# Weight units of the hybrid decoder step split, signalled and released in two parts

## What is computed

```python
def layer(x, ...):
    h = rmsnorm(x, norm_mix)
    q, k, v, g_ret, x_lru, y_lru, g_a, g_b = jnp.split(h @ w_in, IN_SPLITS, axis=-1)
    o, S_new = retention(rope(q), rope(k) * RET_DK ** -0.5, v, S_ret)      # 4 heads, chunked
    ret_branch = (silu(g_ret) * groupnorm(o) * gn_gain) @ w_ret_out
    hl, h_last = rg_lru(causal_conv(x_lru, ...), ...)                      # a scan over time
    lru_branch = (gelu(y_lru) * hl) @ w_lru_out
    x = x + (sigmoid(g_a + b0) * ret_branch + sigmoid(g_b + b1) * lru_branch) @ w_o
    gu = rmsnorm(x, norm_ffn) @ w_gate_up
    return x + (silu(gu[..., :D_FF]) * gu[..., D_FF:]) @ w_down, ...
```

## Time and profile before

| | |
|---|---|
| median of 3 runs | 2520.05 us |
| the profiled execution's own time | 2516.28 us |
| its span in the profile | 2514.3 us |
| TensorE busy with matmuls | 2447.3 us, 97% |
| weight loads on TensorE | 2367.1 us, 94% |
| POOL busy | 1519.6 us, 60% |
| VectorE (DVE) busy | 1213.4 us, 48% |
| ScalarE (ACT) busy | 647.4 us, 26% |
| granted TensorE clock, mean | 0.996 of full speed |

### The profile page before, as it was taken

The page is one execution under the profiler, slowest core; times in us unless marked ns, Lnnn a source line. Parts: engine busy times, 40 slices in busy tenths (PEclk is TensorE's granted clock), DMA queues, the critical chain, the costliest instruction groups (busy, mean ns, idle before and its releaser), DMA issues.

```text
span 2514.3 us, 51834 instructions
## 1 busy us (share of the span) xinstructions
PE 2447.3 (97%) x19636; PEld 2367.1 (94%) x19636; DVE 1213.4 (48%) x1587; ACT 647.4 (26%) x981; POOL 1519.6 (60%) x1265
## 2 busy tenths in 40 slices
PE   7999999999999999999999999999999999999997
PEld 7899989999999999999998989999999999999997
DVE  6745454668644632022347363636786446221223
ACT  2404040446721211011114040413566112100111
POOL 5364536467776666666654545455777666666664
PEclk9999999999999999999999999999999999999998
DMA  5546363522233322332346363635322323223222
GB/s 197 200 147 226 132 237 113 201 86 84 84 97 96 93 92 81 95 92 84 92 159 234 115 240 112 245 126 191 91 77 90 99 92 93 88 84 97 92 83 86
DMA packets 121742, 315.62 MB, mean 126 GB/s; under 512 B 12192, under 2 KB 12960, under 8 KB 121568
## 3 DMA queue, kind: packets, MB, share of 16 engines
q1 hardware_dynamic: 60480, 199.78, 25.4%
q10 hardware_dynamic: 61088, 113.34, 12.8%
HBM read 272.69 MB, written 40.38 MB: 125 GB/s over the span
## 4 chain that ended last, share of the span: by engine, by line
PE 76%; DVE 7%; issue 4%; ACT 3%; DVEq 3%; DMA 3%; ACTq 2%; POOL 1%; POOLq 1%
PE proj L360 46%; PE aux L360 25%; DMA scratch<-in_sret 2%; DVE scratch L1078 2%; PE aux L560 1%; PE aux L534 1%; DVE scratch L988 1%; PE aux L609 1%; POOL w_low L347 1%; POOLq L345 1%; DVE scratch L1136 1%; DMA scratch<-v_rows 1%; ACTq L1338 1%; DVEq L1081 1%; DVEq L996 0%
## 5 line engine op out<-in xcount | busy, mean ns | idle before, releaser
L347 POOL TENSOR_TENSOR w_low<-w_raw,w_high 128x512 fp32r<-128x512 f32 (+2 forms) x840 | 1094.5, 1323 | 62.8 <-issue 1.3
L344 POOL TENSOR_SCALAR w_high<-w_raw 128x1024 fp32r<-128x1024 f32 (+3 forms) x420 | 424.8, 1011 | 907.9 <-PE proj L360 683.0
L360 PE MATMUL proj<-x_high,w_high 128*128 128x260 f32 x2752 | 561.4, 285 | 33.5 <-DVE x_low L751 13.8
L360 PE MATMUL proj<-x_high,w_low 128*128 128x260 f32 x2752 | 555.6, 283 | 0.0
L360 PE MATMUL proj<-x_low,w_high 128*128 128x260 f32 x2752 | 554.8, 283 | 0.0
L360 PEld LDWEIGHTS proj<-x_high,w_high 128*128 128x128 f32 x2752 | 425.5, 189 | 46.0 <-DVE x_low L751 14.2
L360 PEld LDWEIGHTS proj<-x_high,w_low 128*128 128x128 f32 x2752 | 425.4, 189 | 0.0
L360 PEld LDWEIGHTS proj<-x_low,w_high 128*128 128x128 f32 x2752 | 425.1, 189 | 0.0
L360 PE MATMUL proj<-split_scratch,w_high 128*128 128x260 f32 x2544 | 412.3, 284 | 4.4 <-POOL w_low L347 3.3
L360 PEld LDWEIGHTS proj<-split_scratch,w_high 128*128 128x128 f32 x2544 | 348.1, 188 | 13.0 <-issue 5.0
L360 PE MATMUL aux<-x_high,w_high 128*128 128x260 f32 x1344 | 272.0, 283 | 2.6 <-DVE residual L1215 1.4
(11 more groups left out here) (184 smaller groups left out, 2326.3 us busy)
## 6 DMA issues: line engine op xcount, KB each, us to landing
w_raw<-in_wstream SPq DMA_DIRECT2D x252, 512.0 KB, 3.6
scratch<-in_sret ACTq DMA_DIRECT2D x96, 512.0 KB, 6.9
out_ret_s<-scratch ACTq DMA_DIRECT2D x64, 512.0 KB, 3.7
w_raw<-in_wstream SPq DMA_DIRECT2D x72, 448.0 KB, 3.3
w_raw<-in_wstream SPq DMA_DIRECT2D x48, 384.0 KB, 3.0
scratch<-v_rows ACTq DMA_DIRECT2D x64, 256.0 KB, 4.8
w_raw<-in_wstream SPq DMA_DIRECT2D x48, 320.0 KB, 2.8
out_ret_p<-scratch ACTq DMA_DIRECT2D x8, 512.0 KB, 3.4
```

What stands on the lines that cost most here:

```text
L344: pool.tensor_scalar(WH[:, j, w], WR[:, j, w], 1.0, 0.0, ALU.mult, ALU.add)
L347: m = pool.tensor_tensor(WL[:, j, part], WR[:, j, part], WH[:, j, part].bitcast(F32), ALU.subtract)
L360: m = pe.matmul(out, wt[:, w, blk * P:(blk + 1) * P], x[xi], start=first and n == 0, stop=last and n == 2)
```

## The change

Each unit is cut after its first four blocks (`CUT`). POOL makes the high part and then the low part of the first four blocks, signals, and does the same with the rest. `w_split` and `w_used` therefore count parts, two for each unit: TensorE waits for part 0 ahead of block 0 and for part 1 ahead of block 4, and increments `w_used` with the first matmul of block 0 and of block 4. Part `h` of unit `u` may be written once TensorE has begun the part that follows part `h` of unit `u - 2`. SP still transfers whole units, after both parts of `u - 2` are split. The diff, cut to its core (the same second wait stands also in `whole`, `twin`, `ret_out`, `lru_out`, and bases of unit counts are doubled):

```diff
--- before.py
+++ after.py
@@ -36,6 +36,8 @@
 EPS = 1e-6
 UW = 8 * P
 
+CUT = 4
+
@@ -94,6 +96,7 @@
+assert VT == CUT < min(min(blocks) for n, blocks in RUNS)
@@ -319,7 +322,7 @@
                             u = base + k
-                            sp.wait_ge(s["w_split"], layer * UNITS + (u + 1) + i * len(blocks))
+                            sp.wait_ge(s["w_split"], layer * (2 * UNITS) + 2 * (u + 1) + i * (2 * len(blocks)))
                             sp.dma_start(WR[:, u % 2, 0:n * P],
@@ -330,23 +333,23 @@
-            pool.sem_inc(s["w_split"], 2)
+            pool.sem_inc(s["w_split"], 4)
             with pool.Fori(0, DEPTH) as layer:
                 for base, times, blocks in runs():
                     with pool.Fori(0, times) as i:
                         for k, n in enumerate(blocks):
-                            j, w = (base + k) % 2, slice(0, n * P)
-                            u = layer * UNITS + base + k + i * len(blocks)
-                            pool.wait_ge(s["w_used"], u + 2)
-                            pool.wait_ge(w_ld[j], (layer * (UNITS // 2) + i * (len(blocks) // 2)) * 16
-                                         + 16 * ((base + k) // 2 + 1))
-                            pool.sem_inc(s["go_pool"], 1)
-                            pool.tensor_scalar(WH[:, j, w], WR[:, j, w], 1.0, 0.0, ALU.mult, ALU.add)
-                            pool.drain()
-                            for part in (slice(0, n // 2 * P), slice(n // 2 * P, n * P)):
-                                m = pool.tensor_tensor(WL[:, j, part], WR[:, j, part],
-                                                       WH[:, j, part].bitcast(F32), ALU.subtract)
-                            m.then_inc(s["w_split"], 1)
+                            j = (base + k) % 2
+                            u = layer * (2 * UNITS) + 2 * (base + k) + i * (2 * len(blocks))
+                            for h, w in enumerate((slice(0, CUT * P), slice(CUT * P, n * P))):
+                                pool.wait_ge(s["w_used"], u + (h + 2))
+                                if h == 0:
+                                    pool.wait_ge(w_ld[j], (layer * (UNITS // 2) + i * (len(blocks) // 2)) * 16
+                                                 + 16 * ((base + k) // 2 + 1))
+                                pool.sem_inc(s["go_pool"], 1)
+                                pool.tensor_scalar(WH[:, j, w], WR[:, j, w], 1.0, 0.0, ALU.mult, ALU.add)
+                                pool.drain()
+                                pool.tensor_tensor(WL[:, j, w], WR[:, j, w], WH[:, j, w].bitcast(F32),
+                                                   ALU.subtract).then_inc(s["w_split"], 1)
@@ -354,7 +357,7 @@
             def product(outs, w, blk, xs, first, last):
-                started = blk
+                started = blk % CUT
@@ -373,8 +376,8 @@
-            def unit_begin(ub, u):
-                pe.wait_ge(s["w_split"], ub + (u + 3))
+            def unit_begin(ub, u, part=0):
+                pe.wait_ge(s["w_split"], ub + (2 * u + part + 5))
@@ -416,6 +421,8 @@
                 unit_begin(ub, u)
                 for k in range(MT):
+                    if k == CUT:
+                        unit_begin(ub, u, 1)
                     m = product(outs, u % 2, k, pairs(hi, lo, k), k == 0, k == MT - 1)
@@ -423,8 +430,8 @@
                 for k in ks:
-                    if q % size == 0:
-                        unit_begin(ub, u + q // size)
+                    if q % size in (0, CUT):
+                        unit_begin(ub, u + q // size, q % size // CUT)
@@ -441,21 +448,20 @@
-            pe.sem_inc(s["w_used"], 2)
+            pe.sem_inc(s["w_used"], 4)
@@ -725,6 +733,8 @@
                             unit_begin(ub0, u)
                             for b in range(K_DOWN[v]):
+                                if b == CUT:
+                                    unit_begin(ub0, u, 1)
```

More of the change, by code:

```diff
@@ L403, in twin @@
                 for k in range(MT):
-                    if k % (MT // 2) == 0:
-                        unit_begin(ub, u + k // (MT // 2))
+                    if 2 * k % CUT == 0:
+                        unit_begin(ub, u + k // (MT // 2), 2 * (k % (MT // 2)) // CUT)
                     pe.wait_ge(made, count + (k + 1))
@@ L450, in _ @@
             with pe.Fori(0, DEPTH) as layer:
-                ub0, tb0 = layer * UNITS, layer * TILES + TILE0
+                ub0, tb0 = layer * (2 * UNITS), layer * TILES + TILE0
                 def ret_out(hh, ub, u0, tb, i0, behind=None):
                     for m_ in range(MT):
-                        if m_ % 2 == 0:
-                            unit_begin(ub, u0 + m_ // 2)
+                        unit_begin(ub, u0 + m_ // 2, m_ % 2)
                         tile_begin(tb, i0 + m_)
@@ L499, in one_head @@
                     else:
-                        ub, tb = ub0 - MT // 2 + head * U_HEAD, tb0 - MT + head * T_HEAD
+                        ub, tb = ub0 - MT + head * (2 * U_HEAD), tb0 - MT + head * T_HEAD
                         uv, v0 = QK + MT // 2, QK + MT
@@ L690, in _ @@
                     for j in range(4):
-                        place = (ub0 + 12 * i, B_MERGE + 3 * j, MG_UNIT)
+                        place = (ub0 + 24 * i, B_MERGE + 3 * j, MG_UNIT)
                         n, q = R_MERGE + 3 * j, 0
@@ L718, in _ @@
                         for j in range(4):
-                            single(ub0 + 4 * i, bu + 2 + j, ring_begin(layer, n0 + 2 + j, i), XH, XL)
+                            single(ub0 + 8 * i, bu + 2 + j, ring_begin(layer, n0 + 2 + j, i), XH, XL)
                     for m_ in range(MT):
```

## The result

| | before | changed |
|---|---|---|
| median (runs) | 2519.20 us (4: 2517.57 to 2520.45) | 2493.66 us (4: 2490.25 to 2494.29) |
| ratio | | 0.9897 [0.9885, 0.9909] |
| profiled execution | 2516.28 | 2494.29 |
| its span, mean granted clock | 2514.3 | 2492.5, 0.996 |

The change is worth 25.5 us on the medians and 22.0 between the two profiled executions. The direction is the forecast one.

What follows compares the result with a forecast made beforehand. TensorE was taken as the bound, matmuls in flight for 97% of the span, so only its idle time could be won. Stalls of 8.2 and 8.3 us by layer gave -16.5, other terms 0: 2520.05 to 2503.5 us, range 2496 to 2513.

Steps and rivals of the forecast that it cites:

- The stalls behind POOL: TensorE waiting for POOL's `w_low` at unit starts, plus the late weight load; all should go, -16.5 us.
- the list: Stalls counted in RG-LRU, down products, second gate/up start and unit at 538 us: 8.2 and 8.3 us by layer.
- g: POOL's gap between two parts when the wait is already satisfied; between 0 and 0.4 us, taken as 0.1.
- the second wait: TensorE's extra wait ahead of block 4, 420 more in all; already satisfied and so free, 0 us.
- More work on POOL at no cost: 420 more TENSOR_SCALARs and drains, about 150 us, fit in POOL's 900 us of idle time.
- Losses that do not count: TensorE's stalls from 546 to 622 us, behind DVE's and ACT's chain: 5.0 us over both layers, taken as no gain.
- the losses behind DVE are gained too: Rival: DVE's chain moves up by TensorE's earlier work or is held less; 2498.5 us, chance 0.10.
- DVE's chain shorter by over 2 us: Sign of being wrong: DVE's chain of 81 us between `read_x` waits longer or shorter by over 2 us.
- The estimate of 23 us of holding: In the 65.4 us DVE works in its chain, about 35%, 23 us, is being held up; scan 1879 against 1225 ns.
- The anchor: Profiled execution, 2516.3 us, 3.8 us under the runs' median; the forecast takes 16.5 us off the median 2520.05.
- POOL becomes the bound: Rival in the RG-LRU stretch: at g = 0.35 POOL needs 73.2 against 69.6 us; 2511 us, chance 0.16.
- DVE held longer: Rival where DVE binds: POOL's busy time up 5%, +1.1 us a layer, up to +8; 2515 us taken, chance 0.09.

Runs made afterwards that it cites:

- Signal_only: Changed kernel, but POOL waits for whole units to be given back; parts still made and signalled one by one: 2491.59 us, ratio 0.9889 to the kernel before.
- release_only: Changed kernel, but TensorE waits for both parts before a unit's first block; POOL still starts part 0 early: 2501.02 us, ratio 0.9928.
- Pieces_only: Kernel before, whole-unit waits and signals, each POOL instruction cut into four blocks and the rest, one drain: 2545.90 us, ratio 1.0109.
- no_low: Changed kernel without low weight parts; the third product takes the high part again, matmuls equal in number: 2470.47 us, ratio 0.981.
- low_256: Changed kernel with each TENSOR_TENSOR (low part) cut into pieces of at most two blocks: 2487.22 us, ratio 0.9881.
- order_only: Kernel before, whole-unit waits and signals, POOL making high, drain, low for four blocks, then for the rest: 2549.47 us, ratio 1.0125.
- High_by_block: Changed kernel with high parts made one block at a time, up to three more TENSOR_SCALARs a part: 2529.28 us, ratio 1.0045.

## Why the prediction was wrong, point by point

- **The stalls behind POOL: right.** All of the list went, at every place, 17.3 us for the 16.5 forecast. Signal_only and release_only show that they went for the stated reason, latency ahead of the signal: the work of POOL grew by 112 us and the stalls disappeared.
- **g and the second wait: right.** g measured -0.03 us, nothing, where 0.1 was taken; no unit shows a stall at block 4.
- **More work on POOL at no cost: right, with its condition.** Pieces_only shows 28 us of cost where the signal stays at the unit's end. The cover is the two-part signal and not the 900 us of idle time as such.
- **"Losses that do not count": this step failed.** It took DVE's chain as fixed and gave nothing for the 2.5 us a layer that TensorE loses behind it. The chain became 2.2 us shorter in each layer, so TensorE's earlier arrival at its end was nearly all gained: 4.4 us. This was the case "the losses behind DVE are gained too", given 0.10, and "DVE's chain shorter by over 2 us" stood among the prediction's own signs of being wrong. The step also had a rule for it beside the numbers: the Trainium skill ("SBUF — State Buffer", Who interferes with whom) says that DVE and GpSimd hold their shared port for a whole instruction. What the runs show agrees with it: without POOL's TENSOR_TENSORs DVE's busy time in the chain is 22.9 us less (no_low), and with them in pieces of 256 columns 10.1 us less than in the changed kernel (low_256). What shortened the chain is that the parts of it that lie on DVE were held less, 45.4 to 44.1 us, and its ends, 2.5 to 1.6; ACT's parts did not move (32.6). The pieces do this also under the signals of before: 40.9 us in pieces_only and 42.1 in order_only, where the chain stays long for TensorE's lateness. With the same pieces in the same order DVE's parts measure 42.1, 43.0, 44.0 and 44.1 under the four ways of signalling, so it matters too which instructions meet. Why these values and not others was not found.
- **The estimate of 23 us of holding: met, but not all of it on the chain.** No_low shows 22.9 us. Of these, 16.5 lie in DVE's own parts; the rest lies mostly beside ACT, where being held costs nothing until it outlasts ACT.
- **The wait at 871 us: missing in the list.** It is 0.96 us a layer, 1.9 in all. I had searched TensorE's waits for POOL as releaser only. Here POOL held a DVE instruction, DVE freed a tile late, and TensorE waited for DVE. Order_only shows that the order of the pieces removes it.
- **The anchor.** The sum was made against one profiled execution that lay 3.8 us under the median of its own kernel, and the changed kernel's median lies at its profiled execution (2493.66 and 2494.29). Of the 9.8 us between forecast and result, 5.5 lie in the mechanisms and the rest in this scatter. The range's low end, 2.5 us below the rival "gained too", had no room for it; the runs of the kernel before over all comparisons reach from 2514.6 to 2523.6.
- **POOL becomes the bound: did not happen, mechanism real.** High_by_block brings it about, and low_256 its beginning. POOL's busy time in the RG-LRU window of the changed kernel is 65.8 of 74 us, for 619 matmuls.
- **DVE held longer: it happened in the stretch that the rival named, and cost nothing.** In the chain DVE's busy time rose by 2.4 us a layer, from 69.7 to 72.1, where the rival took 1.1, and the chain became shorter all the same, since the longer instructions lay beside ACT's parts. Over the whole program DVE's busy time fell from 1213.4 to 1178.5 us while POOL's rose. Neither engine's busy time is the measure; what counts is which of DVE's instructions are held.

## What to carry to other kernels

Where a producer works in units on a ring and its consumer stalls by tenths of a us at the head of a unit, look at the time from "may start" to the signal, not at the producer's idle share: a signal for the first part hides all of the latency, and the same cut without the signal lengthens it (here -25.5 and +28 us). Before a loss that "lies behind" another engine is set at nothing, ask whether the change alters that engine's own length, above all where the changed engine holds it up. Take such a chain apart into the parts that lie on each engine before reading anything from its length: a chain that stays as long as it was can hide a shorter part behind a new wait. And follow waits one step further: an engine held by the changed one can be the releaser that the view of waits names.

## What the runs showed of the hardware

- **TensorE's clock after idle time.** In the profiled execution of the changed kernel, behind the 2.85 us wait for `read_x` in the second layer, the granted clock is 0.50, the lower level of 1.2 GHz, and pairs of matmuls stand 0.43 us apart in place of 0.24:

```profile
1849.85 0.80 PE L363 MATMUL proj<-x_high,w_high 128*128 128x260 f32 x2 [2.85 <-DVE scratch L1077]
1850.45 0.64 PE L363 MATMUL proj<-x_low,w_high 128*128 128x260 f32 x2
1850.88 0.64 PE L363 MATMUL proj<-x_high,w_low 128*128 128x260 f32 x2
...
1849.00:1854.00 5.00, 4.15 (x19) 4.15 (x20) 4.42 (x7) 1.07 (x4) 2.91 (x4) 0.50 0.02 3
```

  It costs 2.6 us. The same wait in the first layer is not followed by a fall; in the second profile of the same kernel it is the other way round, the first layer's costs 1.5 us and the second's nothing. What decides it was not found. The kernel before has such a fall of 1.6 us at 1259 us, so a net cost of 1.0 us stands in the table above.
- **DVE's chain repeats to a hundredth.** In two profiled executions of the changed kernel it took 78.35 us in all four places, while the same pieces in the same order under other signals, with DVE never idle for TensorE, gave 77.54 (signal_only, both layers) and 78.20 and 78.50 (release_only). So the lengths follow mostly from the program, and scatter explains at most the 0.3 us between the last two.
